# Sums over the values of a latent attention, for two blocks of queries at once as three fp32r passes

## The chip, the cores and the metric

The kernel runs on one core of a Trainium2 chip. The metric is the device time of one execution, in microseconds. Before the change the median of three runs is 3228.4 us (3224.39 to 3231.38).

## The reference

Two layers over 1024 latent and 256 context tokens of width 1024: a retention and convolution mixer, a latent attention, and behind each a mixture of 16 experts. The change lies in the attention of the second layer, of which this is what matters:

```python
MLA_HEADS, MLA_NOPE, MLA_ROPE, MLA_V = 8, 128, 64, 128
MLA_QK = MLA_NOPE + MLA_ROPE
ATTN_BLOCK = 128

def blocked_attention(q, k, v):
    scale = d ** -0.5
    def one(qblk):
        s = jnp.einsum('bhqd,bhkd->bhqk', qblk, k).astype(jnp.float32) * scale
        p = jax.nn.softmax(s, axis=-1)
        return jnp.einsum('bhqk,bhkd->bhqd', p.astype(v.dtype), v)
...
ox = blocked_attention(qx, jnp.concatenate([kx, kc], axis=2), jnp.concatenate([vx, vc], axis=2))
```

q, k and v are fp32, with 8 heads, 1024 queries and 1280 keys (10 tiles of 128); only the latent queries are needed in this layer. Queries and keys go through an RMS norm and a rotary turn of their last 64 columns.

## The kernel before

The program is written by hand, engine by engine: each stage is a block in which TensorE, ScalarE (act), VectorE (dve), GpSimd (pool) and the DMA queue (sp) have an instruction list each, tied by semaphores. Each engine works through its list in order, so what waits holds up all that stands behind it. The stages are the front, the retention, and for each layer the output projection, the routing and the experts; `latent_attention` stands before the second layer's. All matmuls that matter for the result are split: a value a is held as ah + al, ah rounded to fp32r and al = a - ah, and a product takes the three passes ah bh, ah bl, al bh. The sum over the values is the exception: it uses plain fp32.

`latent_attention` first makes the latent rows and the queries and keys of head 0. Then comes the loop over 64 **units** (`units = AH * XT`): unit n is head n // 8 and the 128 query rows of tile n % 8. In **iteration n** TensorE makes the scores of unit n, VectorE and ScalarE do the softmax of unit p = n - 1, and the probabilities of unit m = n - 2 are turned (transposed) and summed over the values. Beside this run 18 **steps** of the next head (8 query tiles, 10 key tiles), as many in the iterations of a head as `BESIDE = [3, 3, 2, 3, 2, 3, 2, 0]` says: steps of queries in iterations 0, 1 and 6, of keys in 2 to 5. The last head has none beside it. The order in each engine's list for one iteration is:

- TensorE: `turn(m, 0)` (4 key tiles, bank 6), first step, `turn(m, 1)` (4 tiles, bank 7), `score(n, 0)` and `score(n, 1)` (512 columns each, 5 passes), second step, `turn(m, 2)` (2 tiles, bank 6), third step, `score(n, 2)` (256 columns), and the sum: 10 fp32 matmuls of 128 columns into bank 7 (L2257).
- ScalarE: the exponential of unit p (L2385), a copy of group 0 of the turned probabilities, for the first step its rounded parts (`place`), a copy of group 1 (L2339), the other steps, and the copy of the sum into `oT` (L2406).
- VectorE: the maximum of unit p (L2529) and its scaling (L2533), `take` of the first step from PSUM bank 5 (L2458) and its `low` parts (L2468, L2471, L2473), the reciprocal and the scaling of the probabilities (L2541, L2543), `take` of the second step, the copy of group 2 (L2482), the second step's `low`, the third step.
- GpSimd: for each step the chain of its norm and rotary turn (`step(make)`; for a key L2619, L2621, L2623, L2626, L2627, for a query L2631 to L2595), begun when ScalarE has its sum of squares (L2333).

A step lags by two: `place(s)` on TensorE turns what GpSimd finished for step s - 2 (L2161) and multiplies for step s (L2170 or L2176). All steps of the loop use PSUM bank 5, so one can't begin before the last has been taken.

## Time and profile before

| what | value |
| --- | --- |
| median of three runs | 3228.4 us |
| the profiled execution, its span | 3223.18 us, 3221.4 us |
| granted TensorE clock over the span | 0.957 |
| TensorE matmul, weight load | 2905.2 us (90%), 2410.8 us (75%) |
| VectorE, ScalarE, GpSimd | 2088.9 us (65%), 1458.4 us (45%), 759.1 us (24%) |
| the sums, L2257, 1280 matmul records | 158.0 us, 279 ns each |

"Busy" of a matmul goes from its start to its modelled end; matmuls overlap, so the distance between two starts is the time that one takes from TensorE, and the 279 ns are longer than that. The loop over the units runs from about 1840 to 2434 us of the span. A wait is the idle time of an engine ahead of an instruction, with the engine that ended it. "Granted clock" is the share of 2.4 GHz.

### The profile page before, as it was taken

The numbers are of one execution on the slowest core, as the hardware profiler recorded it, in microseconds if no ns is written. First come the engines' busy times: TensorE is split into PE (matmuls) and PEld (weight loads), VectorE is DVE, ScalarE is ACT, GpSimd is POOL, SyncE is SP. The second block draws the span as 40 slices with busy tenths as digits, with TensorE's granted clock in tenths as the row PEclk, the third lists the DMA queues.
The fourth block names the chain that finished last, engine by engine and source line by source line (L and its number), as shares of the span: only waits on it lengthen the run. The fifth ranks groups of instructions, "written<-read, shape, count | busy, mean of one in ns | idle before, by whom it ended". The sixth has DMA issues, their size and how long they took to land. (4 is left out here: it accounts for less than half of the span.)

```text
span 3221.4 us, 53995 instructions
## 1 busy us (share of the span) xinstructions
PE 2905.2 (90%) x20680; PEld 2410.8 (75%) x20680; DVE 2088.9 (65%) x2441; ACT 1458.4 (45%) x2151; POOL 759.1 (24%) x1259
## 2 busy tenths in 40 slices
PE   6999997699399999999968899999998859999998
PEld 3767686677388888888857788888887747777776
DVE  3576854744667667667644456555554488888887
ACT  2212113532155555555534344444443246767675
POOL 0000003700012212212224655555510001111111
PEclk8999998999599999999989999999999879999999
DMA  5367725443578778778741000000013379999995
GB/s 224 118 207 252 247 82 198 146 175 126 194 272 305 275 283 309 275 281 311 265 139 43 9 16 16 16 16 16 8 60 130 116 316 363 371 361 370 368 381 183
DMA packets 104500, 631.55 MB, mean 196 GB/s; under 512 B 11969, under 2 KB 28609, under 8 KB 70178
## 3 DMA queue, kind: packets, MB, share of 16 engines
q1 hardware_dynamic: 89762, 591.85, 49.2%
q0 software_dynamic: 14592, 37.76, 4.8%
q8 instruction: 91, 1.49, 0.2%
q14 instruction: 55, 0.45, 0.0%
HBM read 563.41 MB, written 66.16 MB: 195 GB/s over the span
## 5 line engine op out<-in xcount | busy, mean ns | idle before, releaser
L1828 DVE TENSOR_TENSOR ex_wlo<-ring,ex_whi 128x2048 fp32r<-128x2048 f32 x384 | 877.3, 2289 | 269.9 <-ACT ex_whi L1757 266.7
L1757 ACT CAST ex_whi<-ring 128x2048 fp32r<-128x2048 f32 x384 | 727.6, 1904 | 339.6 <-PE psum L1720 255.5
L1720 PE MATMUL psum<-ex_whi,ex_xh 128*128 128x512 f32 x1024 | 409.2, 400 | 0.0
L1720 PE MATMUL psum<-ex_wlo,ex_xh 128*128 128x512 f32 x1024 | 399.2, 390 | 0.0
L1720 PE MATMUL psum<-ex_whi,ex_xl 128*128 128x512 f32 x1024 | 398.9, 390 | 0.0
L469 PE MATMUL psum<-fr_whi,fr_hh 128*128 128x512 f32 x560 | 224.8, 403 | 10.7 <-DVE fr_hl L653 9.1
L1720 PEld LDWEIGHTS psum<-ex_whi,ex_xh 128*128 128x128 f32 x1024 | 192.1, 188 | 49.7 <-issue 8.9
L1720 PEld LDWEIGHTS psum<-ex_whi,ex_xl 128*128 128x128 f32 x1024 | 192.2, 188 | 41.3
L1720 PEld LDWEIGHTS psum<-ex_wlo,ex_xh 128*128 128x128 f32 x1024 | 192.5, 188 | 36.8
L469 PE MATMUL psum<-fr_wlo,fr_hh 128*128 128x512 f32 x560 | 218.4, 392 | 0.7 <-DVE fr_wlo L659 0.7
L469 PE MATMUL psum<-fr_whi,fr_hl 128*128 128x512 f32 x560 | 218.4, 392 | 0.0
L1720 PE MATMUL psum<-ex_whi,ex_hh 128*128 128x512 f32 x512 | 211.6, 413 | 0.0
L1720 PE MATMUL psum<-ex_whi,ex_hl 128*128 128x512 f32 x512 | 202.0, 395 | 0.0
L1720 PE MATMUL psum<-ex_wlo,ex_hh 128*128 128x512 f32 x512 | 201.9, 394 | 0.0
L1618 POOL DMA_INDIRECT x_d<-ring,idx_x x16 | 52.5, 3282 | 604.4 <-DVE ring L1866 604.4
L2458 DVE COPY la_taken<-psum 128x448 f32<-128x448 f32 (+2 forms) x146 | 95.4, 654 | 143.3 <-PE psum L2170 82.9
L714 DVE SCALAR_TENSOR_TENSOR conv_y<-conv_u,fr_taps,conv_y 128x1295 f32<-128x1295 f32 x120 | 180.1, 1560 | 0.0
L1618 POOL DMA_INDIRECT out_x<-ring,idx_x x16 | 52.3, 3270 | 512.7 <-DVE ring L1866 512.7
L2257 PE MATMUL psum<-la_arena,ring 128*128 128x128 f32 x1280 | 158.0, 279 | 9.4 <-DVE la_arena L2482 9.4
L2257 PEld LDWEIGHTS psum<-la_arena,ring 128*128 128x128 f32 x1280 | 148.7, 192 | 16.2 <-DVE la_arena L2482 14.2
L2186 PE MATMUL psum<-la_kh,la_qh 128*128 128x512 f32 (+1 forms) x384 | 146.8, 382 | 0.0
L2186 PE MATMUL psum<-la_kl,la_qh 128*128 128x512 f32 (+1 forms) x384 | 136.5, 355 | 0.0
(295 smaller groups left out, 5919.4 us busy)
## 6 DMA issues: line engine op xcount, KB each, us to landing
ring<-in_moe_w SPq DMA_DIRECT2D x192, 2048.0 KB, 10.2
fr_raw<-in_mod_w SPq DMA_DIRECT2D x40, 1024.0 KB, 5.5
rec_d<-fr_work SPq DMA_DIRECT2D x72, 256.0 KB, 5.8
fr_raw<-in_ev_w_in SPq DMA_DIRECT2D x14, 1024.0 KB, 5.6
ring<-rec_d SPq DMA_DIRECT2D x10, 1024.0 KB, 15.6
h_d<-ring SPq DMA_DIRECT2D x18, 512.0 KB, 2.9
fr_arena<-in_mod_w SPq DMA_DIRECT2D x8, 1024.0 KB, 11.8
ring<-mod_d SPq DMA_DIRECT2D x15, 512.0 KB, 7.7
```

Source lines behind the costliest of these rows:

```text
L469: last = nc.tensor.matmul(g.psum[:, bank(s), :], pairs[n][0][t][:, 4 * b + k, :], pairs[n][1][m % 3][:, k, :], start=(b == 0 and i == 0), ...
L714: nc.vector.scalar_tensor_tensor(conv.y[:, j, :], us, w, conv.y[:, j, :], ALU.mult, ALU.add).then_inc(conv_set[j], 1)
L1618: pool.indirect_dma_start(dst, bass.IndirectOffsetOnAxis(ap=idx[:, e:e + 1], axis=0), src[:, :], None, compute_op=ALU.add).then_inc(done, 16)
L1720: last = nc.tensor.matmul(g.psum[:, 2 + i % 2, :], x[:, 4 * b + k, :], w[n][:, k, :], start=(b == 0 and k == 0 and first == 0), stop=(b == ...
L1757: nc.scalar.copy(whi[m % RING][:, :, :], slot(i)[:, 4 * b:4 * b + 4, :]).then_inc(hi_set, 1)
L1828: nc.vector.tensor_tensor(wlo[n][:, :, :], slot(i)[:, 4 * b:4 * b + 4, :], whi[n][:, :, :].bitcast(F32), ALU.subtract).then_inc(lo_set, 1)
L2186: last = nc.tensor.matmul(score_bank(n, c), q, k[s][:, m, k0:k1], start=(i == 0), stop=(i == len(products) - 1))
L2257: last = nc.tensor.matmul(g.psum[:, 7, 0:P], v[m // XT % 2][:, k, :], pT[:, cols(k)], start=(k == 0), stop=(k == KEYT - 1))
L2458: nc.vector.tensor_copy(taken[:, s % 3, c], g.psum[:, bank(s), c]).then_inc(out_set, 1)
```

## The change

The sums of units m - 1 and m are made together in the iterations with an odd m (so odd n), which then turn and sum 256 columns. Turned probabilities are held as a pair of fp32r tiles for two units, `pTh` and `pTl`, and the values as `vh` and `vl`. ScalarE copies all three groups into `pTh` (which rounds), VectorE subtracts from the PSUM group into `pTl`. For heads 1 to 7 ScalarE writes `vh` where it wrote `v`, and GpSimd writes `vl` at the start of its step; head 0's values are split at once ahead of the loop. TensorE's waits for the turned groups become waits for `pl_set`. The tiles lie in parts of the ring that were free, and `oT` moves. The core of the diff, first the tiles and TensorE:

```diff
-        v = [g.ring[:, a + v_at:a + v_at + TOK].rearrange("p (k n) -> p k n", k=KEYT) for a in sets]
+        vh = [ringed(f"vh{s}", [P, KEYT, P], free[s] + 2 * TOK) for s in range(2)]
+        vl = [ringed(f"vl{s}", [P, KEYT, P], sets[s] + v_at) for s in range(2)]
+        pTh, pTl = (ringed(n, [P, KEYT, 2 * P], free[m]) for m, n in enumerate(("pTh", "pTl")))
...
+        def prob_part(x, m, j):
+            k0, k1 = groups[j]
+            return x[:, k0:k1, m % 2 * P:(m % 2 + 1) * P]
+
+        def prob_bank(j):
+            k0, k1 = groups[j]
+            return g.psum[:, 6 + j % 2, 0:(k1 - k0) * P].rearrange("p (k n) -> p k n", n=P)
...
                     if m >= 0:
                         pe.wait_ge(normed, m + 1)
                         if m:
-                            pe.wait_ge(copied_v, m)
+                            pe.wait_ge(pl_set, 3 * m)
                         turn(m, 0)
...
-                        if m:
-                            pe.wait_ge(o_set, m)
+                        if m >= 2:
+                            pe.wait_ge(o_set, m // 2)
                         turn(m, 1)
...
-                        pe.wait_ge(copied_a, 2 * m + 1)
+                        pe.wait_ge(pl_set, 3 * m + 1)
                         turn(m, 2)
...
-                    if m >= 0:
-                        pe.wait_ge(copied_v, m + 1)
-                        pe.wait_ge(copied_a, 2 * m + 2)
+                    if m >= 0 and m % 2:
+                        h = m // XT
+                        pe.wait_ge(pl_set, 3 * m + 3)
+                        if h:
+                            pe.wait_ge(vl_set, KEYT * h)
+                        else:
+                            pe.wait_ge(first_vl, 1)
                         for k in range(KEYT):
-                            last = nc.tensor.matmul(g.psum[:, 7, 0:P], v[m // XT % 2][:, k, :], pT[:, cols(k)],
-                                                    start=(k == 0), stop=(k == KEYT - 1))
+                            for i, (a, b) in enumerate(((vh, pTh), (vl, pTh), (vh, pTl))):
+                                last = nc.tensor.matmul(g.psum[:, 7, 0:256], a[h % 2][:, k, :], b[:, k, :],
+                                                        start=(k == 0 and i == 0), stop=(k == KEYT - 1 and i == 2))
                         last.then_inc(summed, 1)
```

ScalarE, in `place(s)`, in `copy(m, j)`, ahead of the loop and in it:

```diff
-                            nc.scalar.copy(v[h % 2][:, t, :], taken[:, turn % 3, P:2 * P])
+                                nc.scalar.copy(vh[h % 2][:, t, :], taken[:, turn % 3, P:2 * P]).then_inc(vh_set, 1)
...
-                        nc.scalar.copy(pT[:, 512 * j:512 * j + 512], g.psum[:, 6 + j, :]).then_inc(copied_a, 1)
+                        nc.scalar.copy(prob_part(pTh, m, j), prob_bank(j)).then_inc(ph_set, 1)
...
+                nc.scalar.copy(vh[0][:, :, :], first_v).then_inc(first_vh, 1)
...
-                        act.wait_ge(turned, 3 * m + 1)
-                        if m:
-                            act.wait_ge(summed, m)
+                        if m >= 2:
+                            act.wait_ge(summed, m // 2)
                         copy(m, 0)
-                    for j, s in enumerate(hd.beside[n] if n < units else []):
+                    beside = hd.beside[n] if n < units else []
+                    for s in beside[0:1]:
                         place(s)
...
+                    copy(m, 1)
+                    for s in beside[1:2]:
+                        place(s)
+                    copy(m, 2)
+                    for s in beside[2:3]:
+                        place(s)
...
-                    if m >= 0:
+                    if m >= 0 and m % 2:
                         h, t = divmod(m, XT)
-                        act.wait_ge(summed, m + 1)
+                        act.wait_ge(summed, m // 2 + 1)
...
-                        nc.scalar.copy(oT[h % 2][:, cols(t)], g.psum[:, 7, 0:P]).then_inc(o_set, 1)
+                        nc.scalar.copy(oT[h % 2][:, (t - 1) * P:(t + 1) * P], g.psum[:, 7, 0:256]).then_inc(o_set, 1)
```

VectorE, in `take(s)`, the subtraction, and its places in the loop:

```diff
+                        if keys_up_to(s - 2):
+                            dve.wait_ge(vl_set, keys_up_to(s - 2))
...
-                def copy(m, j):
-                    k0, k1 = groups[j]
-                    dve.wait_ge(turned, 3 * m + j + 1)
-                    if m:
-                        dve.wait_ge(summed, m)
-                    nc.vector.tensor_copy(pT[:, k0 * P:k1 * P], g.psum[:, 6 + j % 2, 0:(k1 - k0) * P]).then_inc(copied_v, 1)
+                def low_prob(m, j):
+                    dve.wait_ge(ph_set, 3 * m + j + 1)
+                    nc.vector.tensor_tensor(prob_part(pTl, m, j), prob_bank(j), prob_part(pTh, m, j).bitcast(F32),
+                                            ALU.subtract).then_inc(pl_set, 1)
...
                     for s in beside[0:1]:
                         take(s)
+                    if m >= 0:
+                        low_prob(m, 0)
                     for s in beside[0:1]:
                         low(s)
...
-                        copy(m, 2)
+                        low_prob(m, 1)
...
                     for s in beside[2:3]:
                         take(s)
+                    if m >= 0:
+                        low_prob(m, 2)
+                    for s in beside[2:3]:
                         low(s)
```

GpSimd, at the head of `step(make)`:

```diff
+                    turn = hd.turn(make)
+                    if turn is not None and hd.steps[turn][0] == "k" and hd.steps[turn][1]:
+                        _, h, t = hd.steps[turn]
+                        pool.wait_ge(vh_set, keys_up_to(turn + 1))
+                        nc.gpsimd.tensor_tensor(vl[h % 2][:, t, :], taken[:, turn % 3, P:2 * P],
+                                                vh[h % 2][:, t, :].bitcast(F32), ALU.subtract).then_inc(vl_set, 1)
```

The order of the instructions, without times, at two places. First VectorE in iteration 6 of a head (two steps beside), before and then after; `la_taken` is a step's product taken from PSUM, `ring` holds the softmax statistics, `la_arena` the probabilities.

```order
L2529 TENSOR_REDUCE ring<-psum 128x1
L2533 TENSOR_SCALAR ring<-ring 128x1
L2458 COPY la_taken<-psum 128x448
L2468 TENSOR_TENSOR la_kl_9503<-la_taken,la_kh_9501 128x2x128
L2541 RECIPROCAL ring<-ring 128x1
L2543 TENSOR_SCALAR la_arena<-la_arena,ring 128x1280
L2458 COPY la_taken<-psum 128x448
L2482 COPY la_arena<-psum 128x256
L2468 TENSOR_TENSOR la_kl_9503<-la_taken,la_kh_9501 128x2x128
```

```order
L2562 TENSOR_REDUCE ring<-psum 128x1
L2566 TENSOR_SCALAR ring<-ring 128x1
L2490 COPY la_taken<-psum 128x448
L2511 TENSOR_TENSOR la_pTl<-psum,la_pTh 128x4x128
L2500 TENSOR_TENSOR la_kl_9503<-la_taken,la_kh_9501 128x2x128
L2576 RECIPROCAL ring<-ring 128x1
L2578 TENSOR_SCALAR la_arena<-la_arena,ring 128x1280
L2490 COPY la_taken<-psum 128x448
L2511 TENSOR_TENSOR la_pTl<-psum,la_pTh 128x4x128
L2500 TENSOR_TENSOR la_kl_9503<-la_taken,la_kh_9501 128x2x128
L2511 TENSOR_TENSOR la_pTl<-psum,la_pTh 128x2x128
```

The copy of the third group (L2482 before), which stood behind the second take, has gone. A subtraction into `la_pTl` (L2511) stands behind the first take, one behind the second take, and one as the last of the round, behind the second step's low part (L2500).

Second TensorE in an iteration 2, from its last turn into the next iteration, before and then after.

```order
L2194 MATMUL psum<-ident,la_arena 128x128 x2
L2186 MATMUL psum<-la_kh_9502,la_qh_9498 128x256
L2186 MATMUL psum<-la_kl_9504,la_qh_9498 128x256
L2186 MATMUL psum<-la_kh_9502,la_ql_9500 128x256
L2186 MATMUL psum<-la_kh_9502,la_qh_9498 128x256
L2186 MATMUL psum<-la_kl_9504,la_qh_9498 128x256
L2257 MATMUL psum<-la_arena,ring 128x128 x10
L2194 MATMUL psum<-ident,la_arena 128x128 x4
L2161 MATMUL psum<-ident,la_taken 128x128 x2
L2176 MATMUL psum<-la_ukvh,la_ckh 128x256
```

```order
L2212 MATMUL psum<-ident,la_arena 128x128 x2
L2204 MATMUL psum<-la_kh_9502,la_qh_9498 128x256
L2204 MATMUL psum<-la_kl_9504,la_qh_9498 128x256
L2204 MATMUL psum<-la_kh_9502,la_ql_9500 128x256
L2204 MATMUL psum<-la_kh_9502,la_qh_9498 128x256
L2204 MATMUL psum<-la_kl_9504,la_qh_9498 128x256
L2212 MATMUL psum<-ident,la_arena 128x128 x4
L2179 MATMUL psum<-ident,la_taken 128x128 x2
L2194 MATMUL psum<-la_ukvh,la_ckh 128x256
```

The 10 matmuls of the sum (L2257) between the last scores (L2186, after: L2204) and the next turn (L2194, after: L2212) have gone from this place; the 30 of the pair (L2280) stand at the same place of the odd iterations.

## Rows read from the trace of the kernel before

**Rows 1.** Windows of one head and of the last head: length, busy us, clock, DMA.

```profile
2061.34:2139.04 77.70, 73.26 (x522) 67.42 (x521) 46.02 (x85) 36.68 (x105) 45.62 (x106) 1.00 0.05 16
2370.30:2422.71 52.41, 52.41 (x362) 46.31 (x361) 25.43 (x40) 21.14 (x40) 0.00 (x0) 1.00 0.24 92
```

**Rows 2.** TensorE's waits in the loop: us, times, longest.

```profile
PE psum L2161 <- POOL la_taken L2627: 18.2, 14, 1.3
PE psum L2257 <- DVE la_arena L2482: 9.4, 23, 2.0
```

**Rows 3.** Timeline, TensorE, end of an iteration: start, length, engine, line.

```profile
2100.54 0.28 PE L2186 MATMUL psum<-la_kh,la_qh 128*128 128x256 f32 x1
...
2101.01 0.28 PE L2186 MATMUL psum<-la_kl,la_qh 128*128 128x256 f32 x1
2101.13 2.39 PE L2257 MATMUL psum<-la_arena,ring 128*128 128x128 f32 x20
2103.36 0.60 PE L2194 MATMUL psum<-ident,la_arena 128*128 128x128 f32 x4
```

**Rows 4.** Groups of the loop by line and form: busy us, mean ns.

```profile
L2339 ACT COPY la_arena<-psum 128x512 f32<-128x512 f32 x128 | 72.2, 579 | 0.5 <-PE psum L2194 0.5
...
L2458 DVE COPY la_taken<-psum 128x512 f32<-128x512 f32 x70 | 48.4, 691 | 58.5 <-PE psum L2176 58.0
...
L2468 DVE TENSOR_TENSOR la_kl<-la_taken,la_kh 128x256 fp32r<-128x256 f32 x70 | 30.8, 441 | 42.5 <-ACT la_kh L2327 42.5
...
L2327 ACT CAST la_kh<-la_taken 128x256 fp32r<-128x256 f32 x70 | 28.1, 401 | 0.0
...
L2333 ACT ACTIVATE ring<-la_taken 128x128 f32<-128x128 f32 x70 | 21.5, 307 | 0.0
...
L2473 DVE TENSOR_TENSOR la_qh<-la_taken,la_qh 64x128 fp32r<-64x128 f32 x50 | 16.5, 329 | 0.7
...
L2449 DVE TENSOR_TENSOR la_ukvl<-la_ukv,la_ukvh 128x512 fp32r<-128x512 f32 x6 | 4.2, 693 | 2.6 <-ACT la_ukvh L2315 2.6
```

**Rows 5.** Timeline, VectorE, one unit of the last head.

```profile
2378.58 0.16 DVE L2541 RECIPROCAL ring<-ring 128x1 f32<-128x1 f32 x1 [2.39 <-ACT la_arena L2385]
2378.78 0.89 DVE L2543 TENSOR_SCALAR la_arena<-la_arena,ring 128x1280 f32<-128x1280 f32 x1
...
2380.99 1.49 DVE L2529 TENSOR_REDUCE ring<-psum 128x1 f32<-128x1280 f32 x1 [0.17 <-PE psum L2186]
2382.51 0.21 DVE L2533 TENSOR_SCALAR ring<-ring 128x1 f32<-128x1 f32 x1
```

**Rows 6.** Timeline, ScalarE, the same unit.

```profile
2376.87 0.27 ACT L2406 COPY la_arena<-psum 128x128 f32<-128x128 f32 x1 [3.93 <-PE psum L2257]
2377.03 1.43 ACT L2385 ACTIVATE la_arena<-psum,ring 128x1280 f32<-128x1280 f32 x1
```

**Rows 7.** Timeline, TensorE: a query's product; first and last turn of a key iteration.

```profile
2077.60 1.47 PE L2170 MATMUL psum<-ring,la_cq 128*128 128x192 f32 x8
...
2112.02 0.60 PE L2194 MATMUL psum<-ident,la_arena 128*128 128x128 f32 x4
...
2117.07 0.38 PE L2194 MATMUL psum<-ident,la_arena 128*128 128x128 f32 x2
```

**Rows 8.** Timeline, GpSimd, chains of key steps.

```profile
2107.42 1.05 POOL L2621 TENSOR_TENSOR la_taken<-la_taken,la_gq 128x128 f32<-128x128 f32 x1
...
2110.45 0.26 POOL L2619 TENSOR_SCALAR ring<-ring,la_pse 128x1 f32<-128x1 f32 x1
2110.67 0.46 POOL L2621 TENSOR_TENSOR la_taken<-la_taken,la_gq 128x128 f32<-128x128 f32 x1
...
2112.44 0.60 POOL L2627 TENSOR_SCALAR la_taken<-la_kbase,ring 128x128 f32<-128x128 f32 x1
```

**Rows 9.** Ten us with a low clock; the first sum.

```profile
1810.00:1820.00 10.00, 6.70 (x30) 6.16 (x29) 4.00 (x8) 2.84 (x12) 7.52 (x22) 0.67 0.00 1
...
1855.72 3.32 PE L2257 MATMUL psum<-la_arena,ring 128*128 128x128 f32 x20 [1.98 <-DVE la_arena L2482]
```

More of the change, by code:

```diff
@@ L1992, in latent_attention @@
         prob = [arena[:, b * TOK:(b + 1) * TOK] for b in range(2)]
-        pT = arena[:, 2 * TOK:3 * TOK]
-        oT = [arena[:, 3 * TOK + s * SEQ:3 * TOK + (s + 1) * SEQ] for s in range(2)]
+        oT = [arena[:, 2 * TOK + s * SEQ:2 * TOK + (s + 1) * SEQ] for s in range(2)]
         cq = tile("cq", [P, XT, QL])
@@ L2026, in latent_attention @@
         ukv_in, kvh_set, kvl_set = sem("ukv_in"), sem("kvh_set"), sem("kvl_set")
-        made, out_set, sq_set, chain, hi_set, lo_set = (sem(n) for n in (
-            "made", "out_set", "sq_set", "chain", "hi_set", "lo_set"))
+        made, out_set, sq_set, chain, hi_set, lo_set, vh_set, vl_set = (sem(n) for n in (
+            "made", "out_set", "sq_set", "chain", "hi_set", "lo_set", "vh_set", "vl_set"))
+        first_vh, first_vl = sem("first_vh"), sem("first_vl")
         scored, max_raw, max_set, exp_set, inv_set, normed = (sem(n) for n in (
             "scored", "max_raw", "max_set", "exp_set", "inv_set", "normed"))
-        turned, copied_a, copied_v, summed, o_set = (sem(n) for n in ("turned", "copied_a", "copied_v", "summed", "o_set"))
+        turned, ph_set, pl_set, summed, o_set = (sem(n) for n in ("turned", "ph_set", "pl_set", "summed", "o_set"))
         o_out = sem.pair("o_out")
@@ L2043, in first_col, with keys_up_to @@
             return 64 if hd.steps[s][0] == "q" else 0
+        def keys_up_to(s):
+            return sum(1 for step in hd.steps[:max(s, 0)] if step[0] == "k" and step[1])
         def turned_to(s):
@@ L2082, in store @@
                 def store(h):
-                    sp.wait_ge(o_set, XT * (h + 1))
+                    sp.wait_ge(o_set, XT // 2 * (h + 1))
                     settle(sp, g)
@@ L2323, in place @@
                             if h >= 2:
-                                act.wait_ge(summed, XT * (h - 1))
-                            nc.scalar.copy(v[h % 2][:, t, :], taken[:, turn % 3, P:2 * P])
+                                act.wait_ge(summed, XT // 2 * (h - 1))
+                            if h:
+                                nc.scalar.copy(vh[h % 2][:, t, :], taken[:, turn % 3, P:2 * P]).then_inc(vh_set, 1)
+                            else:
+                                nc.scalar.copy(first_v[:, t, :], taken[:, turn % 3, P:2 * P])
                         dst = (qh if kind == "q" else kh)[h % 2]
@@ L2521, in _ @@
                     low(s)
+                dve.wait_ge(first_vh, 1)
+                nc.vector.tensor_tensor(vl[0][:, :, :], first_v, vh[0][:, :, :].bitcast(F32), ALU.subtract).then_inc(first_vl, 1)
                 for n in range(units + 2):
```

9 lines of the change are left out of this document (4 added, 5 removed).

## The prediction

> **What bounds the kernel now.** The change touches one stage, the latent attention of layer 1, and in it the loop over 64 units (8 heads of 8 blocks of 128 query rows). I read the windows first, to see whether TensorE is full there; then its waits; then the pace of its instructions; last the other engines' rows, as lengths for a layout of the new order. In the window of one whole head TensorE is busy 73.26 of 77.70 us, and in the last head, which has no steps of a next head beside it, 52.41 of 52.41, at the full granted clock [rows 1]. VectorE is busy 46.02 of 77.70. The first window goes from the output copy of one unit to that of the same unit of the next head, so a head takes 77.7 us. TensorE's idle time in it, 4.4 us, is mostly waits for a step that GpSimd has to finish (18.2 us over the loop, 14 times 1.3) and for turned probabilities before a sum (9.4) [rows 2]. So today TensorE's own work sets the pace, and a cheaper sum is worth its whole length, as long as nothing else begins to wait.
>
> **The sum itself.** What counts is the distance between starts, since matmuls are pipelined. The sum of one unit starts at 2101.13 and what follows it at 2103.36: 2.23 us for 20 records (10 fp32 matmuls of 128 columns, two records each). An fp32r matmul of 256 columns starts every 0.117 us (0.47 for four from 2100.54 to 2101.01) [rows 3]. Two units cost 2 x 2.23 = 4.46 us now and 30 x 0.117 = 3.52 us after, a gain of 0.94 us a pair, 3.8 a head, 30 us over 32 pairs. The Trainium skill (TensorE: Matmul & The Clock Gate, "Back-to-back issue gap") gives 262 cycles for 256 columns, 109 ns at the full clock; by that estimate the 30 would cost 3.28 us and the gain would be 8 us larger over the loop. The row is 8% slower and I take the row.
>
> **What is added, unit by unit.** ScalarE copies all three groups of turned probabilities (now two: 0.579 us for 512 columns [rows 4]; the third, 256 columns, between 0.27 for the 128 of an output copy [rows 6] and 0.579, 0.37 taken). VectorE, which copied the third group, subtracts all three: 512 columns take 0.69 in the one row of that form and size, 256 columns 0.44 [rows 4], and the copy of 256 columns that goes is taken as the same 0.44, so 2 x 0.69 = 1.38 us more a unit. Busy time would allow it: 46.0 + 8 x 1.38 = 57 us of a head of 74. The order does not, because each engine works in program order. Three new dependences matter. (1) The subtraction of group 0 stands on VectorE between the maximum and the reciprocal, and needs ScalarE's copy, which stands behind the exponential. (2) The third group shares PSUM bank 6 with the first group of the next unit, so the next unit's first turn waits for a subtraction that stands last in VectorE's round. (3) The sum comes only in odd iterations, and waits for that same subtraction. In an even iteration the 2.23 us of the sum, which used to give the other engines time, are gone.
>
> **Laid out from the rows.** Lengths [rows 4 to 6]: maximum 1.49 and its scaling 0.21; exponential 1.42; ScalarE copy 0.58; reciprocal and scaling of the probabilities 0.16 + 0.89; a take 0.69; a query step's two low parts about 0.33 each, a key step's 0.44; about 0.04 from one engine's end to the next one's start, 0.2 from TensorE's next start back to the end of a step's data.
> (a) First turn behind an even iteration. From the start of the turn that follows the second step, it is 0.2 to the end of the step, and then VectorE has take 0.69, subtraction 0.69, low part 0.44 to 0.66, subtraction 0.44: with the handovers 2.75. TensorE has turn 0.25 and scores 0.6. It waits 1.9 us, in iterations 3, 5 and 7 of a head. Behind iteration 0, whose third step comes later, 0.2 + 0.69 + 0.44 + 0.06 less scores 0.6 gives 0.8. Sum 6.4 us a head; none of it exists today.
> (b) The sum. After the third step: 0.2 + 0.69 + 0.44 + 0.06 less 0.6 = 0.75 us, three times; in iteration 7, with no steps, reciprocal and scaling 1.13, subtractions 0.73 and 0.47 less 0.85: 1.5. Sum 3.7.
> (c) The third step of iterations 3 and 5. TensorE comes to it 5.05 + 0.25 us behind the first turn (2112.02 to 2117.07, and the turn) [rows 7] and waits 1.3 today. After: VectorE starts the maximum only when TensorE starts the turn (both waited for the same subtraction), so 1.49 + 0.25 + 1.42 + 0.1 + 0.58, then ScalarE's part of the step 0.27 + 0.40 + 0.31 [rows 4, 6] and GpSimd's chain of 2.6 us, or 3.2 where its product meets VectorE's scaling [rows 8]: 7.4 to 8.0, a wait of about 2.3. In iterations 0 and 1 the third step waits for the take of the second: 0.2 + 0.69 less the turn's 0.25, 0.6, in iteration 0; in iteration 1 the round begins 0.6 late and 0.6 + 1.77 + 2.1 + 0.73 + 0.7 + 1.13 + 0.73 = 7.8 stand against 6.5 on TensorE (5.3, and 0.6 for each of two query steps, whose product lasts 1.47 [rows 7] against some 0.86 for six matmuls of 256 columns): 1.3. Sum 6.5. (d) In iteration 7 the last turn waits for group 0's subtraction: 0.9 (a late maximum behind the 0.69 of the next weights' low parts) + 1.77 + 2.1 + 0.73 = 5.4 against TensorE's 3.2: 2.2.
> A head: 77.7 - 4.4 of old waits - 3.8 of cheaper sums + 6.4 + 3.7 + 6.5 + 2.2 = **88.3 us, 10.6 more**; seven heads 74.
> (e) The last head has no steps, so its pace can be followed all the way round. From the subtraction of group 0 in an odd iteration: 1.13 + 0.73 + 0.46 + 0.06, sum 3.52, its end 0.27, output copy 0.37 (ScalarE stands waiting for the sum, as it does for 3.93 us now [rows 6], and the exponential is behind it), exponential 1.5, copy 0.6, subtraction 0.73 = 9.4; then 1.13 + 0.73 + 0.47 + maximum 1.53 + 0.25 + 1.5 + 0.6 + 0.73 = 6.9. A pair takes 16.3 us against 2 x 6.55 (52.41 over 8): 3.2 more, four times, 13.
> (f) The values. ScalarE's copy becomes a rounding of the same size, and GpSimd's new subtraction of 128 columns (0.46, or 1.05 beside VectorE's scaling [rows 8]) fits between it and the square that GpSimd waits for (0.40 + 0.31 us later): nothing, with 14 x 0.5 = 7 us as the upper bound. (g) The start and the end. The first head's values are split before unit 0, 1280 columns on ScalarE and then VectorE, 1.4 + 1.5 by the rows of that width (the exponential, the maximum), half hidden by the first scores: +1.5. The tail of two iterations without scores: about +1.8. The first pair has no unit to turn and so none of the waits above: -2.5. Together +1.
> Sum: 74 + 13 + 1 = 88 us. The profiled execution took 3223.2 us, so 3311; the median of the runs shown is 5 us above that execution, which the range holds.
>
> **Rivals.** *Sums are paid in full* (the other side): if the third subtraction were over before TensorE comes to the next first turn, the loop would keep its waits and lose 30 us: 3193. For it speaks that VectorE has 31.7 us of slack a head; against it that this slack lies in waits for TensorE, ahead of the very takes that the subtraction stands behind. It decides at one number: VectorE would have to need less than 0.85 us for the four operations of (a), which have 0.69 + 0.69 + 0.44 + 0.44 = 2.26 us of busy time. *Only the firm waits*: (a) and (e) need no layout of a whole head. If (b), (c), (d) were covered by each other: 7 x (6.4 - 3.8) + 13 = 31 us, 3255, and 3235 to 3280 with errors. *The clock falls too*: in the stage ahead of the loop, ten us with TensorE busy for 6.70 show a granted clock of 0.67, and the first sum, behind a wait of 1.98 us, took 3.32 us [rows 9] against 2.39 later [rows 3], part of it at 1.2 GHz. Waits near 2 us will come three times a head and in the last head: 25 x 0.9 = 23 us, 3334, more where two fall together. The Trainium skill (same page, "A second HAM failure mode: psum-queue depth-cycling") says that short idle times between groups of matmuls can make the clock swing; by that the higher number would hold, but the waits of 1.3 us in every head leave the clock at 1.00 [rows 1]. *GpSimd becomes the bound*: 7 us at most by (f); part of the range. That the change does not do what it says I leave out: the program's order shows 30 matmuls a pair.
>
> **How the numbers follow.** Forecast (3280 to 3330) 0.56; with the clock 0.15; firm waits alone 0.14; in full 0.10; the two sides cancelling within 0.2% (6.5 us, about what a measurement can tell) 0.05. The range leaves out the last two: it begins between no change and the firm waits, at 3246, and ends at 3350 with the clock's case. Faster 0.10, same 0.05, slower 0.85.
>
> **What would show it.** Right: the sum's line with 960 records 0.117 us apart; heads of about 88 us; TensorE busy some 80% in the head's window; its longest waits for VectorE's subtraction into the low probabilities, before the first turn of iterations 3, 5 and 7 and before every sum; 16.3 us a pair in the last head. Wrong: heads below 77 us, or TensorE still busy over 90% of them; or waits of GpSimd's chain above all.

## The result, and the profile after

The changed kernel takes 3316.2 us (median of four runs, 3312.41 to 3322.85) against 3229.6 for the kernel before on the same chip, a ratio of 1.0282 [1.0265, 1.0299]: 2.8% slower. The profiled execution took 3312.41 us with a granted clock of 0.952. The predicted time was 3311, and its first case, a loop that waits up to three times an iteration pair where TensorE used to be full, is what the profile shows.

The page of the changed kernel, span and busy time of each engine:

```profile
span 3310.3 us, 53496 instructions
## 1 busy us (share of the span) xinstructions
PE 2894.6 (87%) x20360; PEld 2393.0 (72%) x20360; DVE 2161.9 (65%) x2570; ACT 1473.3 (45%) x2184; POOL 798.1 (24%) x1329
```

TensorE is busy for 10.6 us less than before, in a span 88.9 us longer. Windows of one head and of three pairs of the last head, from output copy to output copy as in [rows 1], then the whole loop, from its first score to its last output copy, for the changed kernel and, as the last row, for the kernel before:

```profile
2086.91:2175.81 88.90, 72.23 (x482) 65.34 (x481) 55.15 (x101) 38.16 (x110) 50.99 (x116) 0.98 0.05 14
2457.57:2503.07 45.50, 37.52 (x242) 31.84 (x241) 25.14 (x42) 17.91 (x33) 0.00 (x0) 1.00 0.27 106
1824.80:2518.43 693.63, 560.25 (x3656) 502.43 (x3655) 419.83 (x763) 291.46 (x804) 353.15 (x804) 0.97 0.05 17
...
1829.84:2433.35 603.51, 564.64 (x3976) 516.04 (x3974) 346.83 (x634) 277.83 (x770) 314.54 (x734) 1.00 0.06 20
```

A head takes 88.90 us (77.70 before) and TensorE is busy for 81% of it (94% before). The second window holds three pairs of the last head: 15.2 us a pair, and TensorE, full there before, idles for 8.0 of the 45.5. VectorE is busy for 62% of a head; no engine but TensorE is near full, and TensorE no longer is. TensorE's waits in the loop, from 1840 us on, beside [rows 2]:

```profile
PE psum L2212 <- DVE la_pTl L2511: 63.6, 46, 2.9
PE psum L2179 <- POOL la_taken L2671: 32.5, 13, 2.5
PE psum L2280 <- DVE la_pTl L2511: 18.8, 28, 0.9
PE psum L2179 <- POOL la_taken L2633: 12.2, 7, 1.9
PE psum L2179 <- DVE la_taken L2490: 3.6, 7, 0.6
```

They add up to 130.7 us, where the kernel before had 36.8, so 93.9 more. From the first score to the last output copy the loop takes 693.6 us for 603.5; behind it the program takes 3.8 more (791.9 for 788.05), ahead of it 5.0 less: +90.1 + 3.8 - 5.0 = 88.9, the difference of the spans. The last two say little: over the traces of all the runs below, the first score comes between 1824 and 1833 us and the part behind the loop takes 784 to 798.

TensorE's timeline, the sum of iteration 1 of a head and then iteration 5:

```profile
2108.24 0.39 PE L2280 MATMUL psum<-la_pTh,la_vh 128*128 128x256 f32 x1 [0.58 <-DVE la_pTl L2511]
2108.46 0.28 PE L2280 MATMUL psum<-la_pTh,la_vl 128*128 128x256 f32 x1
...
2111.82 0.28 PE L2280 MATMUL psum<-la_pTl,la_vh 128*128 128x256 f32 x1
2111.94 0.60 PE L2212 MATMUL psum<-ident,la_arena 128*128 128x128 f32 x4
...
2142.11 0.63 PE L2212 MATMUL psum<-ident,la_arena 128*128 128x128 f32 x4 [1.72 <-DVE la_pTl L2511]
...
2147.19 0.38 PE L2212 MATMUL psum<-ident,la_arena 128*128 128x128 f32 x2
2150.07 0.41 PE L2179 MATMUL psum<-ident,la_taken 128*128 128x128 f32 x2 [2.50 <-POOL la_taken L2671]
...
2152.32 0.39 PE L2280 MATMUL psum<-la_pTh,la_vh 128*128 128x256 f32 x1 [0.52 <-DVE la_pTl L2511]
```

The sum lasts from 2108.24 to 2111.94, 3.70 us. From 2142.11 on it is the set of waits of one iteration: 1.72 before the first turn, 2.50 before the third step, 0.52 before the sum. What ended the 1.72 us stands in VectorE's timeline:

```profile
2139.62 0.69 DVE L2490 COPY la_taken<-psum 128x512 f32<-128x512 f32 x1 [0.72 <-PE psum L2194]
2140.22 0.68 DVE L2511 TENSOR_TENSOR la_pTl<-psum,la_pTh 128x512 fp32r<-128x512 f32 x1
2140.98 0.42 DVE L2500 TENSOR_TENSOR la_kl<-la_taken,la_kh 128x256 fp32r<-128x256 f32 x1
2141.54 0.42 DVE L2511 TENSOR_TENSOR la_pTl<-psum,la_pTh 128x256 fp32r<-128x256 f32 x1
2141.88 1.48 DVE L2562 TENSOR_REDUCE ring<-psum 128x1 f32<-128x1280 f32 x1
```

These are the four operations in a row of the prediction's step (a), take, subtraction, low part, subtraction, from 2139.62 to 2141.96, and TensorE's turn starts at 2142.11. The 2.50 us are GpSimd's, in the same iteration:

```profile
2145.91 0.47 POOL L2652 TENSOR_TENSOR la_vl<-la_taken,la_vh 128x128 fp32r<-128x128 f32 x1 [1.60 <-ACT la_vh L2349]
2146.64 0.27 POOL L2663 TENSOR_SCALAR ring<-ring,la_pse 128x1 f32<-128x1 f32 x1 [0.26 <-ACT ring L2359]
2146.87 1.13 POOL L2665 TENSOR_TENSOR la_taken<-la_taken,la_gq 128x128 f32<-128x128 f32 x1
...
2149.33 0.60 POOL L2671 TENSOR_SCALAR la_taken<-la_kbase,ring 128x128 f32<-128x128 f32 x1
```

The new subtraction (L2652) is over 0.26 us before GpSimd has its next input; the chain then starts late because ScalarE did, and its product takes 1.13 us. In the groups of the loop the new work has the lengths that were assumed:

```profile
L2511 DVE TENSOR_TENSOR la_pTl<-psum,la_pTh 128x512 fp32r<-128x512 f32 x127 | 87.0, 685 | 78.5 <-ACT la_pTh L2365 78.4
L2652 POOL TENSOR_TENSOR la_vl<-la_taken,la_vh 128x128 fp32r<-128x128 f32 x70 | 33.5, 479 | 76.7 <-ACT la_vh L2349 76.7
L2511 DVE TENSOR_TENSOR la_pTl<-psum,la_pTh 128x256 fp32r<-128x256 f32 x64 | 26.8, 419 | 2.3 <-ACT la_pTh L2365 0.4
L2365 ACT CAST la_pTh<-psum 128x256 fp32r<-128x256 f32 x64 | 22.8, 357 | 13.5 <-PE psum L2212 13.5
```

And the clock. Two windows of 4 us, from the third step of iteration 3 of the same head on (it starts at 2127.51, behind a wait of 2.49 us):

```profile
2127.00:2131.00 4.00, 3.44 (x18) 3.18 (x19) 1.85 (x4) 0.91 (x4) 3.79 (x9) 0.67 0.01 2
2131.00:2135.00 4.00, 4.00 (x34) 4.00 (x33) 1.21 (x2) 0.41 (x2) 2.31 (x5) 0.91 0.00 0
```

About once in a head, here from about 2128.3 to 2131.7, the granted clock is at its lower level (1.2 GHz) for some 3.4 us; six times this begins within 1.3 us of the end of a wait of 2.5 us. The longest stretch is the last, from 2507.2 to 2517.4, in which TensorE makes the last sum:

```profile
2508.00:2511.00 3.00, 2.27 (x10) 1.86 (x10) 0.96 (x2) 1.17 (x2) 0.00 (x0) 0.50 0.00 0
```

Over the loop the low clock adds up to 44 us, 3.4 before. At half the clock the 41 us more lose 20 at most, less where TensorE idles anyway.

### The profile page after: what moved, and what is told of

It is laid out like the page before. It is cut to its first block and busy times, and to the rows that moved or that the text cites. A ratio compares the mean times of both kernels' runs of the same rounds, so it can differ in the third digit from the quotient of the medians.

```text
span 3310.3 us, 53496 instructions
## 1 busy us (share of the span) xinstructions
PE 2894.6 (87%) x20360; PEld 2393.0 (72%) x20360; DVE 2161.9 (65%) x2570; ACT 1473.3 (45%) x2184; POOL 798.1 (24%) x1329
## 5 line engine op out<-in xcount | busy, mean ns | idle before, releaser
L1720 PEld LDWEIGHTS psum<-ex_wlo,ex_xh 128*128 128x128 f32 x1024 | 192.5, 188 | 36.8
L2511 DVE TENSOR_TENSOR la_pTl<-psum,la_pTh 128x512 fp32r<-128x512 f32 (+1 forms) x192 | 113.2, 596 | 82.2 <-ACT la_pTh L2365 80.2
L2212 PE MATMUL psum<-ident,la_arena 128*128 128x128 f32 x640 | 103.2, 280 | 63.8 <-DVE la_pTl L2511 63.6
L2204 PE MATMUL psum<-la_kh,la_qh 128*128 128x512 f32 (+1 forms) x384 | 148.7, 387 | 0.0
L2204 PE MATMUL psum<-la_kl,la_qh 128*128 128x512 f32 (+1 forms) x384 | 138.1, 360 | 0.0
```

Of the source, the lines that this page charges most:

```text
L1720: last = nc.tensor.matmul(g.psum[:, 2 + i % 2, :], x[:, 4 * b + k, :], w[n][:, k, :], start=(b == 0 and k == 0 and first == 0), stop=(b == ...
L2204: last = nc.tensor.matmul(score_bank(n, c), q, k[s][:, m, k0:k1], start=(i == 0), stop=(i == len(products) - 1))
L2212: last = nc.tensor.transpose(g.psum[:, bank, (k - k0) * P:(k - k0 + 1) * P], prob[m % 2][:, prob_cols(m, k)], g.ident[:, :])
L2511: nc.vector.tensor_tensor(prob_part(pTl, m, j), prob_bank(j), prob_part(pTh, m, j).bitcast(F32), ALU.subtract).then_inc(pl_set, 1)
```

## The experiments

A pair of iterations is given as the distance between output copies, for the iterations 1, 3, 5 and 7 of a head: before 23.0, 19.2, 19.2, 16.3; changed kernel 25.2, 22.5, 21.6, 19.6. "Low clock" is the time at 1.2 GHz from the first score to the last output copy of the run's own trace: 3.4 us before, 44 for the changed kernel. At most half of it is lost. All ratios are to the kernel before, on the same chip. "First turn" is TensorE's wait at L2212, "step" that at L2179, "sum" that at L2280 in the changed kernel.

### What the sum's length is worth

**Subtractions left out (e_nosub).**

```diff
-                            pe.wait_ge(pl_set, 3 * m)
+                            pe.wait_ge(ph_set, 3 * m)
...
-                            for i, (a, b) in enumerate(((vh, pTh), (vl, pTh), (vh, pTl))):
+                            for i, (a, b) in enumerate(((vh, pTh), (vl, pTh), (vh, pTh))):
...
-                    nc.vector.tensor_tensor(prob_part(pTl, m, j), prob_bank(j), prob_part(pTh, m, j).bitcast(F32),
-                                            ALU.subtract).then_inc(pl_set, 1)
+                    pass
```

> The changed kernel without VectorE's subtractions: the low parts of the probabilities are left out (the third pass multiplies the rounded probabilities again, at the same cost), and TensorE waits for ScalarE's copies instead. Theory 'VectorE's added work is the cause': all of the loss goes and the cheaper sums are left, 3195 to 3205. Chain theory: the first turn still waits about 1 us for ScalarE's third copy, and the third step still waits 2.5 us for GpSimd; 5 to 6 us a head less and more in the last head, about 3270, still slower than the kernel before.

Measured: 3269.5 us, 1.0136 [1.0117, 1.0154]. Pairs 24.0, 21.8, 21.8, 17.9; 12.9 in the last head. The chain theory of the expectation had 3270. So VectorE's subtractions account for 47 of the 87 us, and with them gone the kernel still waits for 92.4 us (40.2 for ScalarE's copy before a turn, 48.7 for GpSimd's steps) and is still slower than before.

**One pass of three, on top of that (e_onepass).**

```diff
-                            for i, (a, b) in enumerate(((vh, pTh), (vl, pTh), (vh, pTl))):
+                            for i, (a, b) in enumerate(((vh, pTh),)):
```

> The changed kernel without VectorE's subtractions and with one pass of the three: 10 fp32r matmuls a pair instead of 30, so all low parts are left out. Against the run without subtractions (3270) TensorE has 2.34 us less a pair, 75 us. If a shorter sum were paid in full, 3195; since a shorter sum also lets the even iterations begin sooner, I expect part of it back as waits for steps: 3200 to 3220. If TensorE's work no longer mattered, 3270.

Measured: 3196.1 us, 0.9893 [0.9868, 0.9918], 73.4 less than e_nosub. Twenty matmuls fewer a pair at 0.117 are 2.34 us, 32 pairs 75. TensorE's waits are 100.0 us, hardly more than the 92.4 of e_nosub. A shorter sum is thus still paid in full, even in a loop that waits so much, which was expected only in part: in the timeline of the changed kernel the waits stand ahead of the sum, in its own iteration, and TensorE goes on from the sum without one. The gain that the change was to bring (24 to 28 us, below) was not hidden; it was earned and more than spent elsewhere. It is also the one kernel here that is faster than the kernel before, by 1.1%, and with the sum rounded to fp32r alone.

**The kernel before, with its sums paired and nothing split (e_pair).** Plain fp32, ten matmuls of 256 columns in odd iterations. The diff is to the kernel before.

```diff
-                    if m >= 0:
+                    if m >= 0 and m % 2:
...
+                            last = nc.tensor.matmul(g.psum[:, 7, 0:256], v[m // XT % 2][:, k, :], pT[:, k, :],
+                                                    start=(k == 0), stop=(k == KEYT - 1))
```

> The kernel before with the pairing alone: sums of two units in the odd iterations, still plain fp32, 10 matmuls of 256 columns, the copies of the turned groups shared between ScalarE and VectorE as before, no rounding and no subtraction. TensorE's work stays the same. If the even iterations without a sum are what costs (nothing covers VectorE's and GpSimd's part there), waits rise from 4.4 to 9 to 10 us a head: 3255 to 3275. If only the split costs, 3226.

Measured: 3319.5 us, 1.0285 [1.0267, 1.0303]: the pairing alone costs as much as the whole change, far above what was expected. Its waits and its loop window:

```profile
PE psum L2163 <- POOL la_taken L2633: 43.1, 15, 3.3
PE psum L2196 <- ACT ring L2343: 17.0, 13, 2.1
PE psum L2163 <- POOL la_taken L2601: 14.6, 13, 1.5
PE psum L2196 <- DVE ring L2487: 10.4, 22, 2.1
```

```profile
1830.04:2526.07 696.03, 604.95 (x3336) 527.66 (x3334) 342.46 (x634) 272.52 (x739) 313.74 (x733) 0.92 0.05 17
...
2132.00:2140.00 8.00, 4.75 (x21) 4.18 (x20) 4.29 (x9) 2.25 (x9) 6.05 (x13) 0.64 0.00 1
```

The first row of the second block is the loop, the second the 8 us around one wait of 3.25 us. The loop takes 92.5 us more than before. The waits are 88.6 us, 51.8 more than before, and TensorE is busy for 40.3 us more, although a pair's sum takes 4.32 us at the full clock, no longer than two sums of before. That is the clock's part, some 45 us: 109 us of low clock in 20 stretches for 3.4 in one, at most 0.5 x 106 = 53. So here the clock takes nearly as much as the waits. Behind an iteration without a sum TensorE comes to the next first turn earlier by the length of that sum. In iteration 5 the turn starts at 2126.78; TensorE's own work lasts 5.5 us from there, while the third step, which waits for GpSimd, comes at 2135.49, 8.7 us after the turn. The wait of 3.25 us was 1.3 before [rows 2], and the longer sum stands behind it and gives nothing back.

**The split, without the pairing (e_split).** The changed kernel's copies and subtractions are all there, but every iteration sums its own unit with ten fp32 matmuls of 128 columns.

```diff
-                    if m >= 0 and m % 2:
+                    if m >= 0:
...
-                                last = nc.tensor.matmul(g.psum[:, 7, 0:256], a[h % 2][:, k, :], b[:, k, :],
-                                                        start=(k == 0 and i == 0), stop=(k == KEYT - 1 and i == 2))
+                            last = nc.tensor.matmul(g.psum[:, 7, 0:P], vh[h % 2][:, k, :].bitcast(F32),
+                                                    pTh[:, k, m % 2 * P:(m % 2 + 1) * P].bitcast(F32),
+                                                    start=(k == 0), stop=(k == KEYT - 1))
```

> The changed kernel with the split's work on ScalarE, VectorE and GpSimd kept, but the sums as before: 10 plain fp32 matmuls of 128 columns for each unit in every iteration (the low parts are made and not used). Every sum must wait about 0.9 us for the last subtraction, as in the run with fp32r sums of single units (58.8 us in 63 sums), and the third steps some 25 us: 3226 less 37 us of old waits plus 87 of new, 3265 to 3285. If the uneven iterations alone were the cause, 3226.

Measured: 3294.8 us, 1.0212 [1.0195, 1.0229], 10 above what was expected. Waits 93.9 us, of them 63.0 before the 64 sums (1.0 each), 19.6 for GpSimd; low clock 10 us. So the split alone (VectorE's subtractions and ScalarE's third copy were not told apart) costs 69 us, the pairing alone 94, and both with the cheaper sum 87. In time the two don't add up, 163 against 87, but in waits they nearly do: 51.8 and 57.1 us more alone, 93.9 together. Of the 76 us between 163 and 87, 15 are thus waits that cover one another (in iteration 5, 0.40 and 3.25 us in e_pair, 1.72 and 2.50 in the changed kernel), 24 to 28 are the cheaper sum, and some 25 are the clock, which took some 45 us in e_pair and at most 20 in the changed kernel. The rest is not attributed. Taken out of the changed kernel, the subtractions are worth 47 us (e_nosub), and the pairing with its cheaper sum some 20 (87 - 69 = 18 by the times, 23 by the ratios).

### The rounding of values, and 128 columns

**No subtraction of values on GpSimd (e_novl).**

```diff
-                            for i, (a, b) in enumerate(((vh, pTh), (vl, pTh), (vh, pTl))):
+                            for i, (a, b) in enumerate(((vh, pTh), ((vh if h else vl), pTh), (vh, pTl))):
...
-                        nc.gpsimd.tensor_tensor(vl[h % 2][:, t, :], taken[:, turn % 3, P:2 * P],
-                                                vh[h % 2][:, t, :].bitcast(F32), ALU.subtract).then_inc(vl_set, 1)
```

> The changed kernel without GpSimd's subtraction for the values of heads 1 to 7: their low parts are left out (the second pass multiplies the rounded values again). The prediction's term (f), nothing: within 4 us of 3316. If GpSimd's added work stands behind its waits (44.7 us instead of 19.7), 14 third steps get 0.5 to 1.0 us earlier: 7 to 14 us less.

Measured: 3316.6 us, 1.0284 [1.0262, 1.0305]: no difference, and the wait for GpSimd in iteration 5 is 2.48 to 2.50 us as before. 33.5 us of new work on GpSimd cost nothing.

**fp32r passes for each unit (e_single).** The three passes of 128 columns in every iteration.

```diff
-                    if m >= 0 and m % 2:
+                    if m >= 0:
...
-                                last = nc.tensor.matmul(g.psum[:, 7, 0:256], a[h % 2][:, k, :], b[:, k, :],
+                                last = nc.tensor.matmul(g.psum[:, 7, 0:P], a[h % 2][:, k, :], b[:, k, m % 2 * P:(m % 2 + 1) * P],
```

> The changed kernel with a sum for each unit, 30 fp32r matmuls of 128 columns every iteration, instead of 30 of 256 every other one: the split without the pairing. If 128 columns cost what the fp32 transposes of 128 columns cost, 0.115 us each, a sum takes 3.45 us against 2.23 of plain fp32 and TensorE has 9.8 us more work a head than before the change, but each iteration has a sum behind which the others catch up: about 90 us a head, 3315 to 3345. If 128 columns cost half of 256, 0.06, a sum takes 1.8 us and the heads come to 77 to 80: about 3240.

Measured: 3414.0 us, 1.0586 [1.0569, 1.0604]. TensorE's timeline within one sum:

```profile
2113.75 0.27 PE L2280 MATMUL psum<-la_pTl,la_vh 128*128 128x128 f32 x1
2113.86 0.28 PE L2280 MATMUL psum<-la_pTh,la_vh 128*128 128x128 f32 x1
...
2116.20 0.41 PE L2280 MATMUL psum<-la_pTh,la_vh 128*128 128x128 f32 x1
2116.41 0.42 PE L2280 MATMUL psum<-la_pTh,la_vl 128*128 128x128 f32 x1
2116.63 0.42 PE L2280 MATMUL psum<-la_pTl,la_vh 128*128 128x128 f32 x1
```

With 128 columns the starts are 0.11 us apart, as good as the 0.117 of 256 columns: half the work costs the same, and a sum of 30 lasts 3.4 us. That is why the change pairs units at all. The last three rows show what the lower clock does to the same matmuls, 0.21 apart. The price of the sum came out as expected, the time did not: it was 69 us above the upper end. Against the changed kernel a pair's sums cost 6.8 us for 3.7 (+99 over the loop), TensorE idles for 90.5 us for 133.4 (-43), and low clock is 106 us for 44 (+31 at most); these make +87 at most, and the loop takes 85.1 us more (778.7 for 693.6). (The medians differ by 98 us; the rest lies ahead of the loop and behind it, and in the profiled execution of e_single being the fastest of its four.) The expectation left the clock out.

### Can a better order remove the waits

**Banks exchanged in odd units (e_bank).** The first turn no longer shares its bank with the third group before it.

```diff
-            return g.psum[:, 6 + j % 2, 0:(k1 - k0) * P].rearrange("p (k n) -> p k n", n=P)
+            return g.psum[:, 6 + (j + m) % 2, 0:(k1 - k0) * P].rearrange("p (k n) -> p k n", n=P)
...
-                            pe.wait_ge(pl_set, 3 * m)
+                            pe.wait_ge(pl_set, 3 * m - 1)
```

> The changed kernel with the two PSUM banks of the turned groups exchanged in odd units (7, 6, 7 instead of 6, 7, 6), so that TensorE's first turn no longer waits for VectorE's last subtraction; only the second turn does, behind the first step. Theory 'each wait is worth itself': the wait of 1.6 to 1.7 us in front of the first turn of iterations 3, 5 and 7 and the 0.7 of iteration 1 go, some 4.5 us a head and 31 us in all, 3285. Theory 'one chain': that wait only shadows VectorE's round, whose maximum starts no earlier; the wait comes back in front of the third step (2.5 us becomes about 4) and of the last turn of iteration 7, and the time stays within 5 us of 3316.

Measured: 3336.9 us, 1.0358 [1.0332, 1.0384]. Two waits of the pair of iteration 5, to be held against the 1.72 and 2.50 of the changed kernel:

```profile
2133.76 0.63 PE L2212 MATMUL psum<-ident,la_arena 128*128 128x128 f32 x4 [0.67 <-DVE la_pTl L2513]
2142.67 0.66 PE L2179 MATMUL psum<-ident,la_taken 128*128 128x128 f32 x2 [3.21 <-POOL la_taken L2673]
```

The first wait lost 1 us and the second gained 0.7; pairs whose clock stays high have the changed kernel's lengths (25.2 and 22.3). The wait moved to where the same chain ends next. But with the longer waits came more low clock, 109 us in 23 stretches for 44 in 10, up to 32 us lost, and the kernel is 20 us slower. The expectation of one chain had the places of the waits right and the time wrong (within 5 us of 3316): it left out the clock.

**Output copy behind the exponential (e_out).**

```diff
+                    if m >= 2 and m % 2 == 0:
+                        out(m - 1)
...
-                    if m >= 0 and m % 2:
-                        h, t = divmod(m, XT)
-                        act.wait_ge(summed, m // 2 + 1)
```

> The changed kernel with ScalarE's copy of the output pair moved behind the next exponential, so that the exponential no longer stands behind TensorE's sum. In the last head the exponential leaves the path from the sum to the next subtraction: about 1.1 us a pair, 15.16 becomes 14.0, some 5 us with the tail. If the long stand of ScalarE in front of the output copy (138 us in all) cost time everywhere, each pair would gain about 2.4 us, 77 us in all. I expect the first, 3308 to 3313, since beside the steps of a next head VectorE waits for TensorE in the even iterations anyway.

Measured: 3312.0 us, 1.0259 [1.0233, 1.0286]. As expected only the last head changes, 14.8 us a pair for 15.2 (two pairs in which the clock fell take 16.2); the others stay within 0.05.

**First copy ahead of the exponential in odd iterations (e_copy).**

```diff
+                    def first():
+                        if m >= 2:
+                            act.wait_ge(summed, m // 2)
+                        copy(m, 0)
+
+                    if m >= 0 and m % 2:
+                        first()
```

> The changed kernel with ScalarE's copy of the first turned group put in front of the exponential in odd iterations, where ScalarE stands waiting for the maximum. Chain theory: 0.58 us less in front of GpSimd's chain in iterations 1, 3 and 5, about 0.6 in 7, 2.3 us a head; in the last head copy and subtraction leave the round, 1.2 us a pair: 16 + 5 = 21 us less, 3295. If ScalarE and VectorE were not on the path, nothing.

Measured: 3291.2 us, 1.0193 [1.0167, 1.0219], as expected. Pairs 24.3, 21.2, 21.3, 18.5 and 14.1 in the last head; low clock 17 us. This shortens the chain itself (ScalarE's copy no longer stands behind an exponential of 1.42 us), and 25 us come back (29 by the ratios).

**Steps dealt by the sum (e_beside).** Two steps in the odd iterations, three in the even ones, which have no sum.

```diff
-    BESIDE = [3, 3, 2, 3, 2, 3, 2, 0]
+    BESIDE = [3, 2, 3, 2, 3, 2, 3, 0]
```

> The changed kernel with the steps of the next head dealt out as 3, 2, 3, 2, 3, 2, 3, 0 instead of 3, 3, 2, 3, 2, 3, 2, 0: three in each even iteration, which has no sum, and two in each odd one. Nothing is added or left out. Chain theory: in the measured pairs with two steps and then three the waits are 4.3 to 4.7 us, while behind an even iteration of three the first turn waits 0.7; with no third step in the odd iterations the wait of 2.5 us for GpSimd goes. About 2 us of waits a pair and 3.3 in the last are left, 9 instead of 16.8 a head: 55 us less, 3262. If busy time of VectorE or GpSimd were the cause, the time would stay at 3316.

Measured: 3327.9 us, 1.0318 [1.0299, 1.0336], a clear miss. Where the waits went:

```profile
PE psum L2280 <- DVE la_pTl L2511: 47.8, 32, 2.5
PE psum L2212 <- DVE la_pTl L2511: 45.1, 45, 2.9
PE psum L2179 <- POOL la_taken L2671: 23.4, 27, 2.5
PE psum L2179 <- POOL la_taken L2633: 7.1, 8, 2.2
```

Less waiting for steps (30.5 for 44.7) and for the first turn, but 47.8 us before the sums for 18.8, up to 2.5 each: with fewer steps TensorE comes to the sum earlier and VectorE doesn't. All in all TensorE idles for 128.9 us for 133.4, but low clock rose from 44 to 78 us.

**All of these (e_all), and all but the dealing (e_order).** Both also put VectorE's third subtraction ahead of the second step's low part. e_order has the changed kernel's `BESIDE`.

```diff
+                        low_prob(m, 2)
...
-                    if m >= 0:
-                        low_prob(m, 2)
-                    for s in beside[2:3]:
```

> The changed kernel with the steps dealt out as 3, 2, 3, 2, 3, 2, 3, 0, the first group's copy in front of the exponential in odd iterations, the output copy behind it, and the third group's copy and subtraction in front of the second step's work instead of at the end of the round. Chain theory: some 3.5 us of waits a head are left, 75 us a head against 77.7 of the kernel before, and 13.3 us a pair in the last head: 3205 to 3235, at or below the kernel before (3225).

> The changed kernel with its own dealing of the steps and the three changes of order together: the first group's copy ahead of the exponential in odd iterations, the output copy behind it, the third group's copy and subtraction ahead of the second step's work. The first alone gave 25 us, the second 4; the third should take about 0.5 us from the first turn's wait and from the sum's, where no other chain ends later: 3265 to 3280, the best with three passes, and still slower than the kernel before. If VectorE's round were the only bound, the third would give nothing: 3287.

Measured: e_all 3276.9 us, 1.0163 [1.0142, 1.0183], 42 us above the upper end of what was expected; e_order 3283.5 us, 1.0173 [1.0156, 1.0190], 3 above. (They ran on two chips, where the kernel before took 3226.3 and 3225.6.) e_order idles for 96.3 us against 115.8 in e_copy, 19.5 less, but its low clock is 55 us against 17, up to 19 us lost, and only 8 us are left of the gain (6 by the ratios). e_all and e_order can't be told apart by their ratios, so with the other changes in place the dealing does neither harm nor good. The best order of those tried, e_all, gives back 39 of the 87 us, and the kernel stays 1.6% slower than before.

## Why the prediction was right

**The windows of before** said that a cheaper sum is worth its whole length, and e_onepass shows just that, in the changed loop.

**The sum.** 30 x 0.117 = 3.52 was predicted, 3.70 measured at the full clock: the starts are 0.12 apart, and the first one, behind a wait, takes 0.22. Against two sums of 2.23 us the gain is 0.76 us a pair, 24 for the loop, for 0.94 and 30. But 2.23 was the short one of two lengths: of the 64 sums of before 26 took 2.22 or 2.23 us and 36 took 2.33 or 2.34. By their mean, 2.29, the gain is 0.88 and 28.

**(a) First turn.** 1.62 to 1.72 us in iterations 3, 5 and 7 and 0.67 in iteration 1: 5.7 a head for 6.4 (the terms of the step, 3 x 1.9 + 0.8, make 6.5). The four operations took 2.34 us from first start to last end, in the place and the order that the step named.

**(b) The sum's wait.** 0.58, 0.2 or less, 0.52 and 0.89: 2.0 to 2.2 for 3.7. This term was the most wrong in proportion: in the records VectorE's operations follow each other closer than assumed, as in (e).

**(c) Third step.** 2.50 twice for 2.3 twice, 0.50 for 0.6, and in iteration 1 1.72 for 1.3: 7.2 for 6.5. In iteration 1 the cause given was wrong. It was to be VectorE's take; the trace names GpSimd's chain of a query step (12.2 us, 7 times, in the waits above), the same kind of wait as in the iterations of keys. The rest held: from the start of the first turn at 2142.11 to the third step at 2150.07 are 7.96 us for "7.4 to 8.0".

**(d) Last turn of iteration 7.** 1.71 for 2.2. A head: 88.9 for 88.3, but with 16.7 us of waits for 18.8. What fills the gap is a smaller gain from the sum, and 3.4 us of low clock a head, 1.7 us at most, which the forecast put at nothing.

**(e) Last head.** 15.2 us a pair for 16.3 (e_out 14.8, e_nosub 12.9). The layout added 0.04 us wherever an engine went on to its next instruction. The rows have that where the next one needs the result of the last, as the scaling behind the reciprocal in [rows 5] (2378.58 + 0.16, then 2378.78); where it doesn't, it starts some 0.1 before the end of the last:

```profile
2487.91 0.37 ACT L2436 COPY la_arena<-psum 128x256 f32<-128x256 f32 x1 [4.97 <-PE psum L2280]
2488.18 1.43 ACT L2413 ACTIVATE la_arena<-psum,ring 128x1280 f32<-128x1280 f32 x1
```

The same can be read from [rows 6], 2376.87 + 0.27 against 2377.03. A pair's chain has some eight such places, and 8 x 0.14 = 1.1 us is what is missing; no run tests this by itself. ScalarE's wait for the sum, 3.93 before, is 4.97 now, as described.

**(f) The values** cost nothing (e_novl). **(g) Start and end** were off by more than they are large. From the first score to the first pair's output copy are 43.1 us for 40.6, 2.5 more where 1.0 to 2.5 less was predicted: TensorE waits 2.86 us before a turn there, and 6.8 us are at the low clock. The last pair is 0.2 us longer than the one ahead of it, where before it was 2.5 shorter: 2.7 for 1.8, with the last sum at 1.2 GHz.

**The rivals.** *The clock falls too* came nearly whole: it was worked out at 25 falls of 0.9 us, 23 us; the loop has 10 stretches of low clock, and they cost at most (44.4 - 3.4) / 2 = 20 us. It had a chance of 0.15 and was no part of the forecast. *Paid in full* and *firm waits alone* did not come: the third subtraction is late each time. *GpSimd becomes the bound*: not through its new work, but its old chain, begun later, is what ends 44.7 us of the waits (19.7 before).

**What was luck.** The mechanism was right: the named waits come at the named places, 16.7 us a head for 18.8. The number was as near as it was by errors that cancel. The forecast of 88 us holds 30 us of cheaper sums, so 118 of other terms, nearly all of them waits, and nothing for the clock. Measured are 24 to 28 of sums, 94 of waits and up to 20 of clock: 86 to 90 for the loop's +90.1. So the waits were taken some 24 us too long, and the clock, which was left out, took most of their place.

**What the prediction did not see** is the part of the pairing. It named the time of the sum that is gone from the even iterations, but put (a) down to VectorE's subtractions, and so it would have given the pairing alone little. e_pair shows that the uneven iterations alone cost 94 us, half of it waits and half clock, and e_split that the split alone costs 69. That the sum of (a) to (d) came out near is due to laying out the whole order, not to adding causes.

## What to carry to other kernels

When every engine works through a fixed list, an iteration pair in which the bounding engine's work is moved from one iteration to the other is not neutral: behind the light iteration that engine comes early to a point that the chain through the other engines sets, and the heavy iteration gives nothing back when its added work stands behind that wait. Before pairing work to make it cheaper, compare that chain (8.0 us here from the first turn to the third step) with the bounding engine's own work beside it (5.5): 24 to 28 us were gained and 94 us of new waits bought. And a wait in such a loop is removed only by shortening the chain behind it, as e_copy did; exchanging banks or dealing steps in another way moved it to the next place, and both came with more time at the low clock.

## What the runs showed of the hardware

An fp32r matmul with new weights takes 0.11 us for 128 columns and 0.12 for 256, so passes of 128 columns pay for twice their work. An fp32 sum of the same ten tiles takes 4.32 us for 256 columns and 2.23 to 2.34 for 128: there the time goes with the columns.

The granted clock fell behind waits of very different length: 2.5 us in the changed kernel, 3.2 in e_bank, 1.5 to 1.7 in e_single. In e_split waits of 1.4 to 1.7 us brought no fall at all from 1864 to 2492 us. So the length of a wait alone does not tell whether the clock falls, and what does is not shown by these runs. The clock's share was at most 20 us in the changed kernel and some 45 in e_pair, and it decided between orders: in e_bank TensorE idled less than in the changed kernel (125.4 us for 133.4) and the kernel was 20 us slower, and e_order kept 8 of the 19.5 us by which it idled less. No run changed the clock by itself, so these shares are bounds from the time at the low clock, and in e_pair and e_single also from TensorE's busy time.
